# One pair of expert weight chunks fetched in eleven transfers instead of one

## The reference

```python
xs = jax.vmap(lambda hb, ib: hb[ib])(h, idx)            # 32 tokens for each of 16 experts
a = jnp.einsum('becd,edf->becf', xs, w_gate)            # 1024 -> 2048
u = jnp.einsum('becd,edf->becf', xs, w_up)              # 1024 -> 2048
y = jnp.einsum('becf,efd->becd', jax.nn.silu(a) * u, w_down) * gate[..., None]   # 2048 -> 1024
return jax.vmap(lambda yb, ib: jnp.zeros((n, d), yb.dtype).at[ib.reshape(-1)].add(yb.reshape(-1, d)))(y, idx)
```

## Time and profile before

| | us |
|---|---|
| median of 3 runs (lowest, highest) | 1541.29 (1540.29, 1542.39) |
| the profiled execution's own time | 1540.27 |
| its span in the profile | 1538.5 |
| PE busy, of the span | 1204.2 |
| the queue of SyncE, share of 16 DMA engines' time | 85.1% |

### The profile page before, as it was taken

The page is one execution under the profiler, slowest core; times in us unless marked ns, Lnnn a source line. Parts: engine busy times, 40 slices in busy tenths (PEclk is TensorE's granted clock), DMA queues, the critical chain, the costliest instruction groups (busy, mean ns, idle before and its releaser), DMA issues.

```text
span 1538.5 us, 18557 instructions
## 1 busy us (share of the span) xinstructions
PE 1204.2 (78%) x7530; PEld 698.6 (45%) x7530; DVE 615.3 (40%) x1048; ACT 429.7 (28%) x652; POOL 35.5 (2%) x60
## 2 busy tenths in 40 slices
PE   9999999999999999987666566566565665665665
PEld 7888877887888899622111111111111111111112
DVE  5687789888777867511011011011011011011111
ACT  4665367786564664300000000000000000000001
POOL 0100000010001000000000000000000000000000
PEclk9999999999999999988777677877877777777788
DMA  9876876675755566999999999999999999999996
GB/s 384 323 271 229 299 269 245 227 284 197 284 183 199 219 239 274 409 435 429 433 430 430 433 431 429 432 432 429 429 436 428 429 436 426 432 435 425 434 434 281
DMA packets 40277, 550.12 MB, mean 358 GB/s; under 512 B 5001, under 2 KB 5289, under 8 KB 10497
## 3 DMA queue, kind: packets, MB, share of 16 engines
q1 hardware_dynamic: 37328, 541.08, 85.1%
q0 software_dynamic: 2576, 7.56, 1.5%
q10 hardware_dynamic: 288, 0.30, 0.1%
HBM read 547.84 MB, written 1.61 MB: 357 GB/s over the span
## 4 chain that ended last, share of the span: by engine, by line
PE 47%; DMA 34%; DVE 11%; ACT 3%; issue 3%; DVEq 0%; SPq 0%; ACTq 0%; POOL 0%
PE ps L671 45%; DMA b<-in_w_down 34%; DVE b L1636 5%; PE ps L675 3%; ACT b L1255 2%; DVE b L1653 2%; DVE b L2382 1%; DVE b L2323 1%; ACT b L1257 1%; DMA b<-in_dense 1%; DVE b L2329 1%; DVE b L2361 0%; DVE b L2363 0%; DVE b L1667 0%; ACT L1255 0%
## 5 line engine op out<-in xcount | busy, mean ns | idle before, releaser
L671 PE MATMUL ps<-b,b 128*32 128x512 f32 (+6 forms) x7070 | 1134.1, 536 | 288.0 <-DMA b<-in_w_up 113.3
L671 PEld LDWEIGHTS ps<-b,b 128*32 128x32 f32 (+2 forms) x7070 | 640.8, 158 | 742.5 <-issue 447.7
L1255 ACT ACTIVATE b<-ps 128x512 f32<-128x512 f32 (+4 forms) x169 | 93.4, 553 | 870.6 <-PE ps L671 571.8
L1636 DVE TENSOR_TENSOR b<-b,b 128x1024 fp32r<-128x1024 f32 (+5 forms) x254 | 277.1, 1091 | 95.2 <-ACT b L1255 76.8
L1255 ACT ACTIVATE b<-b 128x1024 fp32r<-128x1024 f32 (+6 forms) x219 | 219.1, 1000 | 191.7 <-PE ps L671 171.6
L2372 DVE TENSOR_TENSOR b<-b,ps 128x512 f32<-128x512 f32 x16 | 11.0, 689 | 391.4 <-issue 378.2
L2382 DVE TENSOR_TENSOR b<-b,ps 128x1024 f32<-128x1024 f32 x28 | 34.2, 1222 | 301.8 <-PE ps L671 301.8
L675 PE MATMUL ps<-b,b 128*128 128x128 f32 (+1 forms) x360 | 70.1, 322 | 37.3 <-DVE b L1667 22.9
L675 PEld LDWEIGHTS ps<-b,b 128*128 128x128 f32 (+1 forms) x360 | 45.8, 168 | 87.6 <-DVE b L1667 36.1
L1653 DVE SCALAR_TENSOR_TENSOR b<-b,b,b 128x512 f32<-128x512 f32 (+3 forms) x50 | 63.2, 1264 | 4.3 <-ACT b L1255 0.5
L1636 DVE TENSOR_TENSOR b<-ps,b 128x512 f32<-128x512 f32 (+8 forms) x73 | 38.3, 524 | 33.1 <-PE ps L671 14.3
(11 more groups left out here) (62 smaller groups left out, 204.2 us busy)
## 6 DMA issues: line engine op xcount, KB each, us to landing
b<-in_w_up SPq DMA_DIRECT2D x29, 4096.0 KB, 43.1
b<-in_w_down SPq DMA_DIRECT2D x29, 4096.0 KB, 38.3
b<-in_w_gate SPq DMA_DIRECT2D x28, 4096.0 KB, 42.9
b<-in_dense SPq DMA_DIRECT2D x88, 1024.0 KB, 5.3
b<-in_w_ada SPq DMA_DIRECT2D x24, 1024.0 KB, 6.9
b<-in_w_gate SPq DMA_DIRECT2D x6, 2048.0 KB, 10.1
b<-in_w_down SPq DMA_DIRECT2D x5, 2048.0 KB, 9.9
b<-in_ada SPq DMA_DIRECT2D x8, 1024.0 KB, 19.0
```

Of the source, the lines that this page charges most:

```text
L671: return e.matmul(o, lhsT, rhs, start=start, stop=stop, skip_group_check=True)
L1255: e.activation(o, i, f, bias=bias, scale=scale).then_inc(mark[0], 1)
L1636: e.tensor_tensor(o, a, b, op).then_inc(mark[0], 1)
```

## The change

In the loop over m, pair 51 is issued by a new function `low_pair`, as eleven transfers. Four times, for j = 0 to 3, come two transfers of eight rows each: partitions j, j+4, ... j+28 with the left half of their row (4096 words, 16 KB), and partitions 32+j, ... 60+j with its first quarter (2048 words, 8 KB). Then come three wider ones: partitions 32 to 63 with the second quarter (8 KB each), partitions 64 to 127 with the left half (16 KB each), and all 128 partitions with the right half (16 KB each). Together they are the same 4 MB in the same places. Each adds 16 to the same semaphore, so the count that TensorE waits for is 160 higher for this pair and every later one in this buffer.

```diff
+E_LOW = 51
+E_LOW_PARTS = 11
...
-            return EP[i][:, g * 4096:(g + 1) * 4096], (S(f"ew{i}"), 16 * (m // E_PAIRS + 2 + (i in E_TWICE)))
+            return EP[i][:, g * 4096:(g + 1) * 4096], (S(f"ew{i}"), 16 * (m // E_PAIRS + 2 + (i in E_TWICE) + (E_LOW_PARTS - 1) * (m >= E_LOW and i == E_LOW % E_PAIRS)))
...
+            def low_pair(n, i):
+                src = pair_src(n)
+                for j in range(4):
+                    e.dma_start(EP[i][j:32:4, 0:4096], src[j:32:4, 0:4096]).then_inc(S(f"ew{i}"), 16)
+                    e.dma_start(EP[i][32 + j:64:4, 0:2048], src[32 + j:64:4, 0:2048]).then_inc(S(f"ew{i}"), 16)
+                e.dma_start(EP[i][32:64, 2048:4096], src[32:64, 2048:4096]).then_inc(S(f"ew{i}"), 16)
+                e.dma_start(EP[i][64:P, 0:4096], src[64:P, 0:4096]).then_inc(S(f"ew{i}"), 16)
+                e.dma_start(EP[i][:, 4096:], src[:, 4096:]).then_inc(S(f"ew{i}"), 16)
...
                 e.wait_ge(S("p_use"), E_PAIR_FREE[m] if m < E_PAIRS else n - 2 * E_PAIRS + 2)
-                if m < pairs - 1:
+                if m == E_LOW:
+                    low_pair(n, i)
+                elif m < pairs - 1:
                     e.dma_start(EP[i], pair_src(n)).then_inc(S(f"ew{i}"), 16)
```

## The result

| | before | after |
|---|---|---|
| median of 5 runs (lowest, highest), us | 1540.50 (1540.25, 1542.39) | 1551.18 (1549.57, 1552.05) |
| the profiled execution's own time, us | 1540.27 | 1551.34 |
| its span, us | 1538.5 | 1549.5 |

The changed kernel takes 1.0065 times as long as the one before, 95% interval 1.0054 to 1.0076: some 10.7 us more by the medians (the table has the five runs of each that were taken side by side), and 11.1 us more for the profiled executions. The forecast was +0.8 us, and its slowest rival +4.25. The lines of the code behind the change have moved by thirteen (L642 of before is L655, L671 is L684).

The account below looks back on a forecast made before the run. The prediction took the experts to be bound by weight transfers, the end by the late DMA engines. Terms +0.6 + 0.2 + 0 + 0 = +0.8 us gave 1542.1 us, from a median of 1541.29; range 1538.9 to 1544.7.

Parts of the forecast that it names:

- What bounds the kernel: Expert stage: bound by weight transfers, 9.71 us a pair; the end hangs on the late half of the DMA engines.
- Term 1: Late engines at pair 51: upper half takes half the rate whoever brings the bytes; -1.82 to +1.21 us, taken +0.6.
- Term 2: Early engines, at the kernel's end: more load and shared-door writes; 0 to +0.8 us beyond the late engines' term, taken +0.2.
- rival 3: At pair 51, the eight engines that get more are the late ones: +4.25 us, 1545.5 us; lower price 1543.1; chance 0.12.
- Rival 1: At pair 51, doors have room and only engine pace counts; late half gains 1.82 us: 1539.5 us; chance 0.26.
- rival 2: At pair 51, the change shifts no load, each engine keeps about 256 KB: time stays 1541.3 us; chance 0.08.
- Term 3: SyncE issuing pair 51: ten more transfers take 4.8 us, covered by some 11 us left; zero, upper bound 0.3 us.
- Term 4: TensorE waiting for all eleven parts of pair 51: makes up a local delay within two pairs; zero.
- below 430 for some microseconds around 1160 to 1172: Sign that the forecast is right: the DMA rate dips below 430 GB/s for some microseconds around 1160 to 1172 us.
- the last landing: Sign that the forecast is right, in the last stretch: the last bytes land at 1527.5 to 1529 us.

Follow-up runs that it names:

- x5: Kernel before plus the change's eight eight-row transfers as an unused extra 768 KB to partitions 0 to 63, in front of pair 51: 1543.84 us, ratio 1.0022.
- x12: Kernel before plus 768 KB extra in eight eight-row transfers, four apart, to partitions 64 to 127, in front of pair 51: 1551.36 us, ratio 1.0067.
- x10: The change applied to pair 6 instead of pair 51, against the kernel before: 1552.88 us, ratio 1.0079.
- x4: The change with its eight eight-row transfers merged into two ordinary ones, five transfers in all, against the kernel before: 1549.55 us, ratio 1.0059.
- x17: Kernel before plus 768 KB extra in eight eight-row transfers, four apart, to partitions 4 to 67, in front of pair 51: 1550.13 us, ratio 1.0058.
- x1: Kernel before with pair 51 as two transfers, partitions 0 to 63 and 64 to 127: 1556.35 us, ratio 1.0106.
- x8: Kernel before plus an extra 1 MB to all 128 partitions in one transfer, in front of pair 51: 1542.92 us, ratio 1.0018.
- x18: Kernel before plus an extra 1 MB to all 128 partitions in eight sixteen-row transfers, spacing eight, in front of pair 51: 1549.61 us, ratio 1.0059.
- x13: Kernel before with pair 51 as sixteen eight-row transfers over all partitions (spacing sixteen), then the rest in one: 1548.26 us, ratio 1.0049.
- x6: Kernel before plus an extra 1 MB to partitions 64 to 127 in one transfer, in front of pair 51: 1550.83 us, ratio 1.0070.
- x9: Kernel before plus an extra 0.25 MB to partitions 64 to 127 in one transfer, in front of pair 51: 1543.39 us, ratio 1.0021.
- x2: Kernel before with pair 51 as two 64-row transfers of every other partition: 1540.54 us, ratio 1.0000.

## Why the prediction was wrong

**Where the 10.7 us are.** Two terms. The low rate costs 9.0 us (3.87 MB, above). The shift of load costs, by an estimate from x5's 3.4 us for 96 KB on each of the eight, half of that for the change's 48 KB: 1.7 us. Together 10.7. That it comes out so exactly is in part luck: the profiled execution, from which the 9.0 us are, lost 11.1. A like sum holds for x12 within 0.1 us: 3.4 + (439 + 424 - 229 - 310) x 10 / 432 = 10.9. For x10 it gives 12.2 against 12.4. But for x4, which has no shift, the rates give 8.3 against 9.2, for x17 the sum is 8.4 against 9.8, and for x1 13.3 against 16. So most of the loss is the low rate, and the split to a tenth of a us isn't shown.

**What bounds the kernel** was right, and so was the place where trouble would show. Since every later stretch hangs on the transfers, a loss there reaches the end whole.

**Term 1 is the step that failed.** It said that an upper half takes half of the rate "whoever brings them", that its bytes are the same as before, and so that only the late engines' 16 KB could be held up: -1.82 to +1.21 us. The runs put another thing in its place. It does matter who brings them (x8 against x18, x5 against x12 and x17), bytes per half do not decide (x13), and the price, 9.0 us in the change, falls on all sixteen engines and on whole-width transfers around, not on the confined bytes (x6, x1). I had seen half of it: the term starts from "the change also alters which engine writes where". But the row I had for it, 326 against 410 GB/s, was read as a full door instead of as engines in each other's way. That load fills 32 partitions only, as a part of x4 does; the row allows both readings, and I followed the cheap one. I also had its place wrong: it is the third of the four loads, which fills partitions 64 to 95, so the 213 GB/s are those of the upper half (the sum is the same). And I had passed over the first of the four, beside which the total was lower still:

```profile
119.60:121.20 1.60, 1.60 (x15) 1.60 (x15) 1.23 (x1) 0.33 (x1) 0.00 (x0) 1.00 1.00 274
```

The bound should have come from the other reading: a lower rate for everything in flight.

**The eight-row transfers**, on which most of the working was spent, are harmless here as to rate; by "own partitions", rows four apart stay with their engines. x5's cause none, and x4 has the low rate without any. In the change that leaves the two wide ones before the last, to partitions 32 to 63 and 64 to 127, as the cause; the second has the rows and the size of x6's extra megabyte. No run has these two alone: x4's two merged transfers are of the suspect kind themselves.

**Term 2 and rival 3.** I took the eight engines for the early ones. x5 shows that the latest engine, or one within some 0.2 us of it, is among them, the point from which rival 3 decides. Its lower price, 1.82 us, agrees with the 1.7 above, which is itself an estimate. Its upper one, +2.43 for shared doors, had the mechanism of term 1 and its size. Rival 1 (-1.8) had the sign of the shift wrong for the same reason, and rival 2 is out, since x5 shows a shift.

**Term 3, SyncE,** held: eleven issues in 7.2 us instead of my 5 to 6, as an eight-row one takes 0.62 us and more, and the busy share never dropped. **Term 4, TensorE,** held too, as the chain still hangs on the transfers.

**Of the signs I had named,** "below 430 for some microseconds around 1160 to 1172" came as 252 and 224 GB/s for 20 us from 1151 on, and the last landing came 10 us after the 1527.5 to 1529 that I gave.

**Open.** Why a write into another engine's partitions slows all sixteen engines, and not two, no run shows. Nor is it shown that it is the write: in every run the source rows were moved with the partitions, so an engine that writes elsewhere reads elsewhere too, and no run separates the two. The load at 152.2 us, which reads from another place and still lowers the total, speaks for the writing side, but it is of another queue. The size is not understood either: at least 128 KB (x9), 512 KB (x6) and 2 MB (x1) are written by engines to which they don't belong, half of what each moves; beyond their bytes they cost 3.0 - 0.6 = 2.4, 10.5 - 2.4 = 8.1 and 16 us. Per byte the small one costs more. How a transfer of 32 or 64 rows is dealt to the sixteen engines was not seen, only that some arrangements cost and some don't. In x10 the low rate itself is larger, (449 + 434 - 205 - 224) x 10 / 432 = 10.5 us against 9.0; why is open, and its interval overlaps with the change's.

## What to carry to other kernels

In a full stream of transfers, as in this kernel, each DMA engine should stay with its own partitions: cut along the free dimension, or take rows that cost nothing extra here (every other partition, or 32 to 95). A block of 64 partitions on one side is to be avoided, since 1 MB so placed cost 9.6 and 10.5 us instead of 2.4, and one of 32 on one side is suspect (x4 has three, never measured alone). A busy share of 1.0 at half of the usual GB/s is the sign of trouble, and it is to be looked for in the transfers around the odd one too. Shifting work between engines by small transfers pays only if the rest of the pair needs no writes outside of the engines' own partitions; here two wide transfers most likely did, and the low rate cost more than the 3.5 us that perfect balance could give.

## What was not expected of the hardware

- All sixteen DMA engines at half speed (213 GB/s, share 0.99, each 32 KB packet 2.33 to 2.56 us instead of 1.21 to 1.23) for over 20 us after two plain transfers of 64 partitions (x1).
- 1 MB over all 128 partitions cost 2.6 us in one transfer and 9.3 us in eight transfers of sixteen rows (x8, x18).
- 768 KB to partitions 0 to 63 in eight-row transfers cost 3.4 us, four partitions higher 9.8 us (x5, x17).
- 64-row transfers to every other partition run at full rate (x2, ratio 1.0000).
- An eight-row transfer takes SyncE 0.62 us and more to issue. A whole-width one takes 0.33 us when nothing was issued just before it, and 0.58 us at the end of the eleven.
